# A decoder layer with a product-key expert block: three of four column chunks of v copied into rows, the fourth gathered in place

## The chip, the cores and the metric

The kernel runs on one core of a Trainium2 chip. The metric is the device time in microseconds (us), the median of the runs. The core's engines are TensorE (PE, with its weight loads PEld), VectorE (DVE), ScalarE (ACT), GpSimd (POOL) and SyncE (SP), which issues most of the DMAs; all DMAs run on the same 16 DMA engines.

## The reference, cut to what matters

The layer has 256 tokens of width 2048. A mixer (two kinds of convolution between two projections) and a layer norm give `x1`; then a block of 16384 experts follows, each with a row of `peer_u` and a row of `peer_v` (2048 columns of float32). Each token picks 16 experts in each of 8 heads, 128 in all:

```
q = (x_tok @ w_q).reshape(t, PEER_HEADS, 2, D_HALF)
s = jnp.einsum('thpc,hpnc->thpn', q, sub_keys)
...                                    # top 16 of each half, top 16 of their sums
experts = e1 * N_KEYS + e2
g = jax.nn.softmax(top_s, axis=-1)
act = jax.nn.gelu(jnp.einsum('td,thkd->thk', x_tok, peer_u[experts]))
return jnp.einsum('thk,thkd->td', act * g, peer_v[experts])
```

The result is added to `x1` and normed again.

## The kernel before, in words

**The stream.** All weights pass through TensorE as units of 512 KB (128 partitions x 1024 float32). There are 656 of them in a fixed order: 80 of `w_in` (units 0 to 79), 32 of `w_out`, 32 of `w_q`, 256 of `u` (units 144 to 399, two for each tile of 128 experts) and 256 of `v` (units 400 to 655). SyncE loads them into a ring of four raw slots (`load`, L424 to L428). ScalarE writes a rounded half `w_hi` (L598), a second engine the rest `w_lo = raw - w_hi`: VectorE (L836), or GpSimd (L521) for some units of `w_out` and all from `w_q` to unit 183. Split units have four slots too. TensorE needs both halves: a unit of the stationary kind is 24 matmuls of 256 columns (L1425 to L1427), a unit of `v` 10 of 512 columns (L1592 to L1597). A load waits until the rest of the unit four before it is made (`lo_done`), and `w_hi` waits until TensorE has used that slot (`used`).

**Beside the stream.** In the `w_in` stage VectorE also does the taps of the convolution (L863 to L876), in the `w_out` stage the norms. In the `w_q` stage and the first of `u` it finds the top 16. From tile 20 of `u` on, VectorE builds one-hot tables (L1213 to L1229) from which TensorE makes the gates of 192 tokens, which are multiplied with the activations of all experts.

**The 64 other tokens.** For these the kernel does not multiply with all of `v`. It gathers the picked rows. Two halves of 64 partitions take four heads each, so there are 64 picks (`PICKS`) of 128 rows. This needs three things:
- `act_spill`: the activations of those tokens, written to DRAM during the `u` stage (L723), and gathered one value per partition (`gather_acts`, L556 to L560).
- `v_rows`: `v` in rows, one expert after the other. The `v` that is loaded lies in units: unit `8g + 2j + h` holds column chunk `j` (512 columns of the 2048) of experts `4g + 2h` and `4g + 2h + 1` for each of the 128 first keys, so an expert's row lies in four pieces of 2 KB. SyncE copies it during the earlier stages, DRAM to DRAM, 512 KB a copy in 256 pieces of 2 KB (`copy_unit`, L442 to L446). `copies_by` (L448) spreads the 256 copies evenly over units 12 to 392 of the stream, in the same queue as the loads: after each load `stream` issues the copies that are due.
- The indices: `selections` (L1259 to L1280) computes on VectorE, once, at tile 24 of `u`, the row of `v_rows` and of `act_spill` for each pick.

**The picks.** GpSimd waits for the indices and for all copies, then gathers the row of a pick, 8 KB on each partition, into one of four buffers (`gather_rows`, L546 to L554), and goes on once the pick four before is done. VectorE adds `coef * row` into `picked` (`pick`, L1287 to L1298), 2048 columns at once, at fixed units of the `v` stage (`pick_unit`): 64 picks over units 420 to 622, one each 3.2 units. The act gathers (16 at first, then four for every three picks) stand between the row gathers in the same queue. `picked` is added near the end.

**Extra loads on SyncE's queue.** `x` in its natural layout (2 MB) after unit 15, the output bias (1 MB) after unit 27, the keys (1 MB) after unit 39, the norm weights (2 x 1 MB) after unit 111, and a spilled `x1` (2 MB) and norm weights (2 x 1 MB) in the `v` stage.

Of the kernel before, what the change touches and what calls it, by code (L numbers as in the profile page):

```python
# [5 lines left out]
P = 128  # L6
T = 256
TB = T // P
D = 2048
# [8 lines left out]
N_KEYS = 128  # L18
DCH = 512
NCH = D // DCH  # L20
GROUP = 4
GROUPS = N_KEYS // GROUP
# [11 lines left out]
PICKS = HEADS * TOPK // HALVES  # L34
ROWS = 4
# [25 lines left out]
U_DOWN = U_UP + 2 * N_KEYS  # L61
# [42 lines left out]

V_UNITS = 2 * NCH * GROUPS
COPY0, COPY1 = 12, U_DOWN - 8


def pick_unit(k):
# [18 lines left out]
def build(nc, x_t, x_nat, w_in, w_out, w_q, u_w, v_w, params, sub_keys, b_out, ln1_g, ln1_b, ln2_g, ln2_b, out):  # L130
    f32 = mybir.dt.float32
# [3 lines left out]
    u32 = mybir.dt.uint32  # L135
    ALU = mybir.AluOpType
# [5 lines left out]
    with ctx:  # L142
        def sb(name, shape, dt, where=ctx):
            return where.enter_context(nc.sbuf_tensor(name, shape, dt))
# [114 lines left out]
        rows = [sb(f"rows{i}", [P, D], f32) for i in range(2)] + rows_late  # L259
        stage = sb("stage", [P, STAGE, SPARSE], f32)  # L260
        picked = sb("picked", [P, D], f32)
        sp_sel = sb("sp_sel", [P, 3, PICKS], f32)
        sp_row = sb("sp_row", [P, 3, PICKS], f32)
        sp_idx = sb("sp_idx", [P, 2, PICKS], u32)
        sp_act = sb("sp_act", [P, PICKS], f32)
        sp_coef = sb("sp_coef", [P, PICKS], f32)
        sp_tok = sb("sp_tok", [P, 2], f32)
# [3 lines left out]
        act_dram = nc.dram_tensor("act_spill", [N_KEYS * N_KEYS * SPARSE, 1], f32, kind="Internal").ap()  # L271
        act_tiles = act_dram.rearrange("(c p t) o -> p c (t o)", c=N_KEYS, p=P, t=SPARSE)

        v_rows = nc.dram_tensor("v_rows", [N_KEYS * N_KEYS, D], f32, kind="Internal").ap()
        v_rows_of = v_rows.rearrange("(p g e) (j c) -> p g e j c", p=P, e=2, c=DCH)

        psum = ctx.enter_context(nc.psum_tensor("psum", [P, 8, DCH], f32))
        bank = [psum[:, i, :] for i in range(8)]
# [102 lines left out]
        sp_chain = sem("sp_chain")  # L381
        idx_done = sem("idx_done")
# [4 lines left out]
        rows_in = [sem(f"rows_in{i}") for i in range(ROWS)]  # L387
# [34 lines left out]
        @block.sync  # L422
        def _(sp):
            def load(slot, src, u=None):  # L424

                if u is not None:
                    wait_lo(sp, u - RAW, slot)
                sp.dma_start(raw[:, slot, :], src).then_inc(raw_in[slot], 16)  # L428

            def load_x(c):  # L430
                sp.dma_start(xt_raw[:, 4 * c:4 * c + 4, :], x_t[:, 4 * c:4 * c + 4, :]).then_inc(xt_in[c], 16)

            load(0, w_in[0])
            load_x(0)
            load_x(1)
            load(1, w_in[1])
            load_x(2)
            load_x(3)
            load(2, w_in[2])
            load(3, w_in[3])  # L440

            def copy_unit(n):  # L442

                g, j, h = n // (2 * NCH), n // 2 % NCH, n % 2
                sp.dma_start(v_rows_of[:, 2 * g + h, :, j, :], v_w[n].rearrange("p (e c) -> p e c", c=DCH))\
                    .then_inc(v_copied[n % 2], 16)  # L446

            def copies_by(u):  # L448

                return V_UNITS * min(max(u - COPY0, 0), COPY1 - COPY0) // (COPY1 - COPY0)  # L450

            def stream(src, base, first, end):
                for n in range(first, end):
                    u = base + n
                    load(n % RAW, src[n], u)
                    for m in range(copies_by(u), copies_by(u + 1)):
                        copy_unit(m)


            stream(w_in, 0, RAW, 4 * RAW)  # L460
            sp.dma_start(acc[:, :, :], x_nat.rearrange("(b p) d -> p b d", p=P)).then_inc(xn_in, 16)
            stream(w_in, 0, 4 * RAW, 7 * RAW)
            sp.dma_start(bo[:, :], b_out.to_broadcast([P, D])).then_inc(bo_in, 16)
            stream(w_in, 0, 7 * RAW, 10 * RAW)
            sp.dma_start(keys[:, :], sub_keys).then_inc(keys_in, 16)
            stream(w_in, 0, 10 * RAW, U_OUT)
            stream(w_out, U_OUT, 0, U_Q - U_OUT)

            for dst, src in ((ln_g, ln1_g), (ln_b, ln1_b)):
                sp.dma_start(dst, src.to_broadcast([P, D])).then_inc(ln1_in, 16)  # L470
            stream(w_q, U_Q, 0, 2 * RAW)
            sp.wait_ge(x1_done, TB * NCH)
            sp.dma_start(x1_dram.rearrange("b p d -> p b d"), acc[:, :, :]).then_inc(x1_out, 16)
            stream(w_q, U_Q, 2 * RAW, U_UP - U_Q)
            stream(u_w, U_UP, 0, U_DOWN - U_UP)
            stream(v_w, U_DOWN, 0, 2 * RAW)
            stream(v_w, U_DOWN, 2 * RAW, 16 * RAW)
            sp.wait_ge(x1_out, 16)
            sp.wait_ge(clo_done, 2 * 6)
            sp.dma_start(res[:, :, :], x1_dram.rearrange("b p d -> p b d")).then_inc(res_in, 16)  # L480
            stream(v_w, U_DOWN, 16 * RAW, 24 * RAW)
            sp.wait_ge(clo_done, 2 * 11)
            for dst, src in ((ln2g, ln2_g), (ln2b, ln2_b)):
                sp.dma_start(dst[:, :], src.to_broadcast([P, D])).then_inc(ln2_in, 16)
            stream(v_w, U_DOWN, 24 * RAW, U_LAST - U_DOWN)
            for j in range(NCH):
                for g in range(G_LAST, GROUPS):
                    for h in range(2):
                        u = down_unit(g, j) + h
                        load(u % RAW, v_w[2 * NCH * g + 2 * j + h], u)  # L490
            for n, (b, d) in enumerate(LN2_VECTOR):
                sp.wait_ge(fin, n + 1)
                sp.dma_start(out[b * P:(b + 1) * P, d * DCH:(d + 1) * DCH],
                             res[:, b, d * DCH:(d + 1) * DCH]).then_inc(out_done, 16)
            sp.wait_ge(out_done, 16 * NCH * TB)
# [3 lines left out]
        def _(pool):  # L499
# [46 lines left out]
            def gather_rows(k):  # L546

                if k >= ROWS:
                    pool.wait_ge(picked_done, k - ROWS + 1)
                elif k >= 2:  # L550
                    pool.wait_ge(used, USED0 + U_DOWN)
                nc.gpsimd.indirect_dma_start(  # L552
                    rows[k % ROWS][:, :], None, v_rows,
                    bass.IndirectOffsetOnAxis(sp_idx[:, 1, k:k + 1], 0)).then_inc(rows_in[k % ROWS], 16)  # L554

            def gather_acts(first, end):  # L556
                for k in range(first, end):
# [6 lines left out]
            for done in v_copied:  # L564
                pool.wait_ge(done, 16 * V_UNITS // 2)
            for k in range(2):
                gather_rows(k)
# [257 lines left out]
        def _(dve):  # L825
            tt = nc.vector.tensor_tensor
            ts = nc.vector.tensor_scalar
            stt = nc.vector.scalar_tensor_tensor
# [105 lines left out]
            with dve.Fori(0, CONF_TILES // 2) as i:  # L934
                for b in range(2):
                    u = U_CONF + 8 * i + 4 * (b + 1) + LEAD
# [20 lines left out]
            with dve.Fori(0, SC_TILES // 4) as i:  # L957
                for b in range(4):
                    u = U_SC + 24 * i + 6 * (b + 1) + LEAD
# [146 lines left out]
            for t in range(2 * HEADS):  # L1106
                h, two = t // 2, t % 2
# [51 lines left out]
            for n, (half, b) in enumerate(decodes):  # L1159
                e = eq[n % 2]  # L1160
# [98 lines left out]
            def selections():  # L1259

                n = [0]

                def then(i):
                    n[0] += 1
                    i.then_inc(sp_chain, 1)

                dve.wait_ge(sp_in, 32)
                dve.wait_ge(tok_done, 1)
                dve.wait_ge(fold_made, 3)
                then(ts(sp_tok[:, 1:2], sp_tok[:, 0:1], float(SPARSE), -float(SPARSE), ALU.is_ge, ALU.mult))  # L1270
                then(stt(sp_row[:, 1, :], sp_sel[:, 0, :], float(N_KEYS), sp_sel[:, 1, :], ALU.mult, ALU.add))
                dve.wait_ge(sp_chain, n[0])
                then(tt(sp_tok[:, 0:1], sp_tok[:, 0:1], sp_tok[:, 1:2], ALU.add))
                dve.wait_ge(sp_chain, n[0])
                then(stt(sp_row[:, 0, :], sp_sel[:, 1, :], float(P * SPARSE), sp_tok[:, 0:1].to_broadcast([P, PICKS]),
                         ALU.mult, ALU.add))
                dve.wait_ge(sp_chain, n[0])
                then(stt(sp_row[:, 0, :], sp_sel[:, 0, :], float(SPARSE), sp_row[:, 0, :], ALU.mult, ALU.add))
                dve.wait_ge(sp_chain, n[0])
                nc.vector.tensor_copy(sp_idx[:, :, :], sp_row[:, 0:2, :]).then_inc(idx_done, 1)  # L1280

            def pick_coefs(n):
                sl = slice(PICKS_IN * n, PICKS_IN * (n + 1))
# [3 lines left out]
            def pick(k):  # L1287

                if k % PICKS_IN == 0:
                    pick_coefs(k // PICKS_IN)  # L1290
                dve.wait_ge(coef_done, k // PICKS_IN + 1)
                dve.wait_ge(rows_in[k % ROWS], 16 * (k // ROWS + 1))
                if k == 0:
                    i = ts(picked[:, :], rows[0][:, :], sp_coef[:, 0:1], None, ALU.mult)
                else:
                    dve.wait_ge(picked_done, k)
                    i = stt(picked[:, :], rows[k % ROWS][:, :], sp_coef[:, k:k + 1], picked[:, :], ALU.mult, ALU.add)  # L1297
                i.then_inc(picked_done, 1)  # L1298
# [23 lines left out]
            for c in range((U_ROUTED - LEAD - U_UP) // 2, N_KEYS):  # L1322
                u = U_UP + 2 * c + LEAD
# [29 lines left out]
            for u in range(U_DOWN, U_END):  # L1353
# [11 lines left out]
                j, n = (u - U_LAST) // (2 * LAST), (u - U_LAST) % (2 * LAST)  # L1365
# [341 lines left out]
```

## Time and profile before

| | |
|---|---|
| median of 3 runs | 1885.39 us (1883.87 to 1888.76) |
| profiled execution, its own time | 1880.05 us |
| its span, first to last instruction | 1878.2 us |
| TensorE busy | 1792.3 us, 12082 matmuls |
| VectorE, ScalarE, GpSimd busy | 1366.5, 852.6, 416.8 us |
| moved by DMA | 568.05 MB, mean 302 GB/s |
| HBM read and written | 558.05 MB and 142.61 MB |

The span is about 2 us shorter than the time of its own execution. Busy shares are means over stages with different limits. Matmuls overlap in the record, so TensorE's pace is better read from how many matmuls started in a stretch. "PEclk" is TensorE's granted clock as a part of full speed.

### The profile page before, as it was taken

How to read it: one execution, taken by the hardware profiler on the slowest of the kernel's cores; microseconds unless marked ns; L12 is line 12 of the kernel's file. 1: busy time of each engine (PE TensorE's matmuls, PEld its weight loads, DVE VectorE, ACT ScalarE, POOL GpSimd, SP SyncE). 2: the span in 40 equal slices, each digit the busy share in tenths (PEclk: the TensorE clock that was granted, in tenths of full speed). 3: DMA queues.
4: the chain of work that ended last, by engine and by line, in shares of the span. 5: the costliest groups of instructions: out<-in, count | busy, mean ns of one | idle time of the engine just before them, and what ended most of it. 6: DMA issues, size and time to landing. Idle time of an engine off the chain costs nothing.

```text
span 1878.2 us, 31945 instructions
## 1 busy us (share of the span) xinstructions
PE 1792.3 (95%) x12082; PEld 1632.6 (87%) x12082; DVE 1366.5 (73%) x1891; ACT 852.6 (45%) x1208; POOL 416.8 (22%) x234
## 2 busy tenths in 40 slices
PE   7989899799999999999999999999999899999997
PEld 7989887599999999999999999988777687777775
DVE  7789886569974677777776444457878788878876
ACT  5434335344444444444444444444445444444443
POOL 0000004468894000000000000033444352222101
PEclk9999999999999999999999999999999999999999
DMA  8999898989989999999999999979899999999874
GB/s 274 308 299 290 270 305 260 316 266 292 288 281 303 308 297 292 308 310 299 291 295 298 314 314 311 312 227 332 337 374 357 360 362 350 337 350 348 298 228 135
DMA packets 196386, 568.05 MB, mean 302 GB/s; under 512 B 35344, under 2 KB 35472, under 8 KB 186512
## 3 DMA queue, kind: packets, MB, share of 16 engines
q1 hardware_dynamic: 167072, 494.20, 81.6%
q0 software_dynamic: 11344, 67.67, 9.3%
q10 hardware_dynamic: 17888, 5.26, 1.2%
q8 instruction: 30, 0.49, 0.1%
q14 instruction: 52, 0.43, 0.1%
HBM read 558.05 MB, written 142.61 MB: 373 GB/s over the span
## 4 chain that ended last, share of the span: by engine, by line
PE 40%; DMA 34%; DVE 11%; ACT 6%; issue 6%; POOL 2%; DVEq 0%; POOLq 0%; ACTq 0%; SPq 0%
DMA raw<-in_u_w_dram 16%; DMA raw<-in_v_w_dram 9%; PE psum L1425 8%; PE psum L1426 8%; PE psum L1427 8%; DVE w_lo L836 6%; DMA raw<-in_w_in_dram 6%; ACT w_hi L598 4%; PE psum L1592 3%; PE psum L1593 3%; PE psum L1594 3%; PE psum L1596 3%; PE psum L1597 3%; POOL w_lo L521 2%; DVE picked L1297 2%
## 5 line engine op out<-in xcount | busy, mean ns | idle before, releaser
L598 ACT ACTIVATE w_hi<-raw 128x1024 fp32r<-128x1024 f32 x652 | 691.3, 1061 | 937.5 <-DMA raw<-in_u_w_dram 259.0
L836 DVE TENSOR_TENSOR w_lo<-raw,w_hi 128x1024 fp32r<-128x1024 f32 x568 | 691.0, 1227 | 371.3 <-ACT w_hi L598 361.8
L1425 PE MATMUL psum<-xt_hi,w_hi 128*128 128x256 f32 x2944 | 834.3, 283 | 35.6 <-DVE w_lo L836 15.1
L1426 PE MATMUL psum<-xt_lo,w_hi 128*128 128x256 f32 x2944 | 826.9, 281 | 0.0
L1427 PE MATMUL psum<-xt_hi,w_lo 128*128 128x256 f32 x2944 | 826.3, 281 | 0.0
L1425 PEld LDWEIGHTS psum<-xt_hi,w_hi 128*128 128x128 f32 x2944 | 558.4, 190 | 42.2 <-issue 17.6
L1426 PEld LDWEIGHTS psum<-xt_lo,w_hi 128*128 128x128 f32 x2944 | 558.5, 190 | 0.0
L1427 PEld LDWEIGHTS psum<-xt_hi,w_lo 128*128 128x128 f32 x2944 | 558.2, 190 | 0.0
L552 POOL DMA_INDIRECT rows<-v_rows,sp_idx x64 | 106.8, 1668 | 922.2 <-DMA v_rows<-in_v_w_dram 615.6
L521 POOL TENSOR_TENSOR w_lo<-raw,w_hi 128x1024 fp32r<-128x1024 f32 x82 | 210.8, 2583 | 86.4 <-ACT w_hi L598 85.8
L1592 PE MATMUL psum<-w_hi,c_hi 128*128 128x512 f32 x504 | 203.5, 404 | 20.6 <-DVE w_lo L836 17.9
L1593 PE MATMUL psum<-w_lo,c_hi 128*128 128x512 f32 x504 | 200.6, 398 | 0.0
L1594 PE MATMUL psum<-w_hi,c_lo 128*128 128x512 f32 x504 | 200.3, 397 | 0.0
L1597 PE MATMUL psum<-w_lo,c_both 128*128 128x512 f32 x504 | 200.1, 397 | 0.0
L1596 PE MATMUL psum<-w_hi,c_both 128*128 128x512 f32 x504 | 200.0, 397 | 0.0
L1297 DVE SCALAR_TENSOR_TENSOR picked<-rows,sp_coef,picked 128x2048 f32<-128x2048 f32 x63 | 147.9, 2348 | 0.1
L1592 PEld LDWEIGHTS psum<-w_hi,c_hi 128*128 128x128 f32 x504 | 95.4, 189 | 53.5 <-DVE w_lo L836 27.7
L1594 PEld LDWEIGHTS psum<-w_hi,c_lo 128*128 128x128 f32 x504 | 95.5, 189 | 23.2
L1596 PEld LDWEIGHTS psum<-w_hi,c_both 128*128 128x128 f32 x504 | 95.4, 189 | 23.3 <-DVE w_lo L836 0.2
L1597 PEld LDWEIGHTS psum<-w_lo,c_both 128*128 128x128 f32 x504 | 95.1, 189 | 23.0
L1593 PEld LDWEIGHTS psum<-w_lo,c_hi 128*128 128x128 f32 x504 | 95.6, 190 | 21.8
L875 DVE SCALAR_TENSOR_TENSOR cacc<-apad,prm,cacc x232 | 101.2, 479 | 0.0
(182 smaller groups left out, 1148.6 us busy)
## 6 DMA issues: line engine op xcount, KB each, us to landing
v_rows<-in_v_w_dram SPq DMA_DIRECT2D x256, 512.0 KB, 9.4
raw<-in_u_w_dram SPq DMA_DIRECT2D x256, 512.0 KB
raw<-in_v_w_dram SPq DMA_DIRECT2D x256, 512.0 KB
raw<-in_w_in_dram SPq DMA_DIRECT2D x80, 512.0 KB
raw<-in_w_out_dram SPq DMA_DIRECT2D x32, 512.0 KB
raw<-in_w_q_dram SPq DMA_DIRECT2D x32, 512.0 KB
act_spill<-stage ACTq DMA_DIRECT2D x32, 128.0 KB, 10.1
xt_raw<-in_x_t_dram SPq DMA_DIRECT2D x4, 512.0 KB, 8.0
```

Of the source, the lines that this page charges most:

```text
L521: nc.gpsimd.tensor_tensor(w_lo[s][:, :], raw[:, s, :], w_hi[s][:, :].bitcast(f32), ALU.subtract).then_inc(lo_done[s], SPLIT)
L598: nc.scalar.activation(parts_of(slot_u)[0][:, :], raw[:, slot_u % RAW, :], ACT.Copy).then_inc(hi_done, 1)
L836: tt(lo_w[:, :], raw[:, slot_u % RAW, :], hi_w[:, :].bitcast(f32), ALU.subtract).then_inc(lo_done[slot_u % SPLIT], SPLIT)
L1297: i = stt(picked[:, :], rows[k % ROWS][:, :], sp_coef[:, k:k + 1], picked[:, :], ALU.mult, ALU.add)
L1425: mm(dst, hi_w[:, sl], xt_hi[:, kk, :], start=st, stop=False)
L1426: mm(dst, hi_w[:, sl], xt_lo[:, kk, :], start=False, stop=False)
L1427: i = mm(dst, lo_w[:, sl], xt_hi[:, kk, :], start=False, stop=en)
L1592: mm(v_bank(j, 0), hi_c[:, n, :], w1, start=st, stop=False)
L1593: mm(v_bank(j, 0), hi_c[:, n, :], w2, start=False, stop=False)
L1594: i = mm(v_bank(j, 0), lo_c[:, n, :], w1, start=False, stop=en)
L1596: mm(v_bank(j, 1), both_c[:, n, :], w1, start=st, stop=False)
L1597: i = mm(v_bank(j, 1), both_c[:, n, :], w2, start=False, stop=en)
```

## The change

Chunk 3 of `v` is no longer copied. `v_rows` holds 1536 columns (6 KB) per expert instead of 2048, and 192 copies instead of 256 are spread over units 24 to 392 instead of 12 to 392. Each pick is gathered by two indirect DMAs on GpSimd: 6 KB per partition out of `v_rows`, and 2 KB per partition out of the units of `v` themselves (`v_ends`, the units seen as rows of 512 columns). `selections` computes a third index for it, `(8g + 6 + h) * 256 + 2 * e1 + e` with `e2 = 4g + 2h + e`, by bit masks. Both gathers of a pick count on one semaphore, so VectorE waits for 32 instead of 16.

```diff
-V_UNITS = 2 * NCH * GROUPS
-COPY0, COPY1 = 12, U_DOWN - 8
+JOINED = NCH - 1
+V_UNITS = 2 * JOINED * GROUPS
+COPY0, COPY1 = 24, U_DOWN - 8
...
-        v_rows = nc.dram_tensor("v_rows", [N_KEYS * N_KEYS, D], f32, kind="Internal").ap()
+        v_rows = nc.dram_tensor("v_rows", [N_KEYS * N_KEYS, JOINED * DCH], f32, kind="Internal").ap()
         v_rows_of = v_rows.rearrange("(p g e) (j c) -> p g e j c", p=P, e=2, c=DCH)
+        v_ends = v_w.rearrange("u p (e c) -> (u p e) c", c=DCH)
...
-                g, j, h = n // (2 * NCH), n // 2 % NCH, n % 2
-                sp.dma_start(v_rows_of[:, 2 * g + h, :, j, :], v_w[n].rearrange("p (e c) -> p e c", c=DCH))\
+                g, j, h = n // (2 * JOINED), n // 2 % JOINED, n % 2
+                sp.dma_start(v_rows_of[:, 2 * g + h, :, j, :],
+                             v_w[2 * NCH * g + 2 * j + h].rearrange("p (e c) -> p e c", c=DCH))\
                     .then_inc(v_copied[n % 2], 16)
...
                 nc.gpsimd.indirect_dma_start(
-                    rows[k % ROWS][:, :], None, v_rows,
+                    rows[k % ROWS][:, 0:JOINED * DCH], None, v_rows,
                     bass.IndirectOffsetOnAxis(sp_idx[:, 1, k:k + 1], 0)).then_inc(rows_in[k % ROWS], 16)
+                nc.gpsimd.indirect_dma_start(
+                    rows[k % ROWS][:, JOINED * DCH:D], None, v_ends,
+                    bass.IndirectOffsetOnAxis(sp_idx[:, 2, k:k + 1], 0)).then_inc(rows_in[k % ROWS], 16)
...
+                then(nc.vector.tensor_copy(sp_u[:, 0, :], sp_sel[:, 1, :]))
...
+                then(nc.vector.tensor_single_scalar(sp_u[:, 1, :], sp_u[:, 0, :], 1, ALU.bitwise_and))
+                then(nc.vector.tensor_single_scalar(sp_u[:, 2, :], sp_u[:, 0, :], 2, ALU.bitwise_and))
...
+                then(nc.vector.tensor_single_scalar(sp_u[:, 0, :], sp_u[:, 0, :], N_KEYS - GROUP, ALU.bitwise_and))
+                dve.wait_ge(sp_chain, n[0])
+                then(nc.vector.tensor_copy(sp_f[:, :, :], sp_u[:, :, :]))
+                dve.wait_ge(sp_chain, n[0])
+
+                then(stt(sp_row[:, 2, :], sp_f[:, 0, :], float(2 * NCH * 2 * P // GROUP), sp_f[:, 1, :],
+                         ALU.mult, ALU.add))
...
+                then(stt(sp_row[:, 2, :], sp_f[:, 2, :], float(P), sp_row[:, 2, :], ALU.mult, ALU.add))
...
+                then(stt(sp_row[:, 2, :], sp_sel[:, 0, :], 2.0, sp_row[:, 2, :], ALU.mult, ALU.add))
+                dve.wait_ge(sp_chain, n[0])
+                then(nc.vector.tensor_scalar_add(sp_row[:, 2, :], sp_row[:, 2, :], float(2 * JOINED * 2 * P)))
+                dve.wait_ge(sp_chain, n[0])
+                nc.vector.tensor_copy(sp_idx[:, :, :], sp_row[:, 0:3, :]).then_inc(idx_done, 1)
...
-                dve.wait_ge(rows_in[k % ROWS], 16 * (k // ROWS + 1))
+                dve.wait_ge(rows_in[k % ROWS], 32 * (k // ROWS + 1))
```

## Rows read from the trace of the kernel before

**Rows 1.** The page, part 1: busy us, share of the span, instructions.

```profile
PE 1792.3 (95%) x12082; PEld 1632.6 (87%) x12082; DVE 1366.5 (73%) x1891; ACT 852.6 (45%) x1208; POOL 416.8 (22%) x234
```

**Rows 2.** Windows: stretch, length, busy us of each engine (instructions), PEclk, DMA share, GB/s.

```profile
700.00:1000.00 300.00, 299.96 (x2574) 297.10 (x2573) 217.09 (x287) 143.77 (x289) 0.00 (x0) 1.00 0.99 301
1000.00:1200.00 200.00, 199.04 (x1695) 198.01 (x1695) 98.61 (x112) 84.34 (x140) 0.00 (x0) 1.00 1.01 305
1300.00:1800.00 500.00, 480.21 (x2016) 379.28 (x2014) 401.75 (x320) 235.45 (x256) 158.39 (x104) 0.99 0.92 344
```

**Rows 3.** Windows of 40 us, engines in the order PE, PEld, DVE, ACT, POOL.

```profile
40.00:80.00 40.00, 38.10 (x309) 37.54 (x308) 32.20 (x59) 17.36 (x18) 0.00 (x0) 0.96 0.99 298
80.00:120.00 40.00, 37.07 (x310) 36.27 (x309) 32.71 (x58) 17.15 (x18) 0.00 (x0) 1.00 1.01 315
120.00:160.00 40.00, 36.24 (x288) 35.28 (x287) 34.74 (x56) 14.00 (x17) 0.00 (x0) 0.96 0.98 291
...
200.00:240.00 40.00, 34.19 (x265) 33.58 (x264) 32.36 (x61) 15.03 (x17) 0.00 (x0) 0.91 0.86 273
...
600.00:640.00 40.00, 39.10 (x337) 38.65 (x336) 27.20 (x42) 19.06 (x37) 0.00 (x0) 1.00 0.99 311
640.00:680.00 40.00, 37.99 (x310) 37.23 (x309) 26.07 (x38) 18.48 (x38) 0.00 (x0) 0.96 0.98 297
```

**Rows 4.** Chain of waits, 84 to 142 us: start, us, what.

```profile
105.04 10.10 DMA raw<-in_w_in_dram
...
119.13 1.15 DVE w_lo L836
120.30 10.31 DMA raw<-in_w_in_dram
```

**Rows 5.** Windows: one slice of the down stage.

```profile
1530.00:1560.00 30.00, 30.00 (x130) 24.17 (x129) 24.37 (x21) 14.21 (x16) 13.58 (x11) 1.00 0.99 382
```

**Rows 6.** DMA issues: count, KB of each, median us from issue to landing.

```profile
v_rows<-in_v_w_dram SPq DMA_DIRECT2D x256, 512.0 KB, 9.4
...
acc<-in_x_nat_dram SPq DMA_DIRECT2D x1, 2048.0 KB, 11.0
```

**Rows 7.** Timeline of VectorE near 205 us: start, us, line, [idle before <-releaser].

```profile
205.32 1.23 DVE L836 TENSOR_TENSOR w_lo<-raw,w_hi 128x1024 fp32r<-128x1024 f32 x1 [0.84 <-ACT w_hi L598]
212.48 0.48 DVE L966 SCALAR_TENSOR_TENSOR scpad<-psum,prm,hval 128x256 f32<-128x256 f32 x1 [5.94 <-issue]
```

**Rows 8.** Waits, 340 to 358 us, then 1190 to 1210: us, times, longest.

```profile
PE psum L1469 <- POOL w_lo L521: 2.7, 2, 1.7
...
PE psum L1425 <- ACT psum L714: 2.5, 1, 2.5
```

**Rows 9.** Timelines of ScalarE and TensorE near 652 us.

```profile
650.97 1.06 ACT L598 ACTIVATE w_hi<-raw 128x1024 fp32r<-128x1024 f32 x1 [3.68 <-DMA raw<-in_u_w_dram]
...
654.74 1.83 PE L1559 MATMUL psum<-oh2g,oh 128*128 128x256 f16 x8 [2.01 <-DVE oh2g L1229]
```

**Rows 10.** Groups (busy us, mean ns, idle before, releaser); last, one line's starts.

```profile
L552 POOL DMA_INDIRECT rows<-v_rows,sp_idx x64 | 106.8, 1668 | 922.2 <-DMA v_rows<-in_v_w_dram 615.6 <-DVE picked L1297 291.1 <-DVE picked L1294 13.6
L558 POOL DMA_INDIRECT sp_act<-act_spill,sp_idx x64 | 81.6, 1275 | 56.2 <-DMA act_spill<-stage 30.1 <-issue 26.2
L1297 DVE SCALAR_TENSOR_TENSOR picked<-rows,sp_coef,picked 128x2048 f32<-128x2048 f32 x63 | 147.9, 2348 | 0.1
...
L1297 DVE SCALAR_TENSOR_TENSOR picked<-rows,sp_coef,picked x63: 2336/2346/2398, 1289.7 to 1782.2; 128x2048 f32<-128x2048 f32 x63
```

**Rows 11.** The page, part 3: queue, packets, MB, share of 16 engines.

```profile
q1 hardware_dynamic: 167072, 494.20, 81.6%
q0 software_dynamic: 11344, 67.67, 9.3%
```

**Rows 12.** One index operation: ns min/median/max, first and last start.

```profile
L1278 DVE SCALAR_TENSOR_TENSOR sp_row<-sp_sel,sp_row x1: 224/224/224, 628.3 to 628.3; 128x64 f32<-128x64 f32 x1
```

**Rows 13.** Timeline of GpSimd: the eighth act gather, [idle before <-releaser].

```profile
1251.93 1.32 POOL L558 DMA_INDIRECT sp_act<-act_spill,sp_idx  x1 [3.35 <-issue]
```

More of the change, by code:

```diff
@@ L263, in build @@
         sp_row = sb("sp_row", [P, 3, PICKS], f32)
-        sp_idx = sb("sp_idx", [P, 2, PICKS], u32)
+        sp_u = sb("sp_u", [P, 3, PICKS], u32)
+        sp_f = sb("sp_f", [P, 3, PICKS], f32)
+        sp_idx = sb("sp_idx", [P, 3, PICKS], u32)
         sp_act = sb("sp_act", [P, PICKS], f32)
@@ L1277, in selections @@
                 dve.wait_ge(sp_chain, n[0])
+                then(stt(sp_row[:, 2, :], sp_f[:, 2, :], float(P), sp_row[:, 2, :], ALU.mult, ALU.add))
                 then(stt(sp_row[:, 0, :], sp_sel[:, 0, :], float(SPARSE), sp_row[:, 0, :], ALU.mult, ALU.add))
                 dve.wait_ge(sp_chain, n[0])
-                nc.vector.tensor_copy(sp_idx[:, :, :], sp_row[:, 0:2, :]).then_inc(idx_done, 1)
+                then(stt(sp_row[:, 2, :], sp_sel[:, 0, :], 2.0, sp_row[:, 2, :], ALU.mult, ALU.add))
[3 more added lines that the diff above has]
+                nc.vector.tensor_copy(sp_idx[:, :, :], sp_row[:, 0:3, :]).then_inc(idx_done, 1)
             def pick_coefs(n):
```

## The prediction

> **What bounds the kernel now.** I read the engine table first. TensorE is busy 95% of the span, so it sets the end, and a change that does not touch its work can win only the time that it stands waiting or runs slow [rows 1]. That share flatters it, because matmuls overlap in the record, so the next view is the number of matmuls per stretch. From 700 to 1000 us, 2574 matmuls started in 300 us, one per 116.6 ns, with the DMA engines at a share of 0.99 [rows 2]. This is the full pace for a 256-column matmul: TensorE has no idle time there although the DMA engines are full. The same view in 40 us slices shows where it falls short of the 343 matmuls that fit at that pace: 309, 310 and 288 from 40 to 160 us, 265 from 200 to 240, 337 and 310 from 600 to 680 [rows 3]. From 1000 to 1200 us it is 1695 of 1716 [rows 2].
>
> The chain of waits says what is late. In the early stretch it is a ring: a load takes 10.10 us from 105.04 on, ScalarE splits the unit, VectorE does taps and then its own half of the split (1.15 us at 119.13), that frees the raw slot, and the next load starts at 120.30 and takes 10.31 us [rows 4]. The ring has four slots, so it feeds a unit each (120.30 - 105.04) / 4 = 3.8 us here, and TensorE wants one each 24 x 0.1166 = 2.8 us. Two thirds of a turn are the load. The loads are slow because the copies stand in the same queue. All 256 copies are 512 KB each, so as many bytes as 256 loads, spread over 380 units (0.67 per unit).
>
> In the down stage there are no copies. 2016 matmuls of 512 columns started from 1300 to 1800 us, and at the 130 per 30 us of the best slice 2167 would fit: 151 x 0.2308 = 34.8 us are lost there, at a DMA share of 0.92 [rows 2, 5].
>
> **Copies: 192 for 256, from unit 24 on.** Per unit this is 192/368 = 0.52 for 0.67. Bytes per unit with its load fall from 1.67 to 1.52 times 512 KB, 9%. With the share at 0.99 and TensorE at full pace before, I expect about 0.9 and loads that arrive ahead, so that up to three split units lie ready and cover a late load. The stretches, one by one:
> - 40 to 160 us: 34 + 33 + 55 = 122 matmuls, 14.2 us [rows 3]. By unit 48 (about 140 us) the copies issued are 24 x 0.52 = 12.5 instead of 36 x 0.67 = 24.3. The 12 that are gone are 6.2 MB, at 298 GB/s some 21 us of the DMA engines. What they were in conflict with are the one-off loads of x (2 MB) [rows 6], the bias and the keys (1 MB each), 4.2 MB or 14 us. So the cause is more than covered. I take 9 us and keep 0 and 14.2: VectorE is over 80% busy here and some gaps are its own.
> - 200 to 240 us: 78 matmuls, 9.1 us, with a low clock in part (0.91). VectorE issued nothing for 5.94 us before its first operation of the next loop [rows 7], released by nothing that the profile shows. The copies did not cause that, but TensorE felt it whole because no split unit was in store. With loads ahead it may be hidden; I take 3, ends 0 and 9.1.
> - 340 to 358 us: TensorE waits 2.7 us for splits of w_out whose loads were late [rows 8]. I take 1.
> - 600 to 680 us: 6 + 33 matmuls, 4.5 us. At 650.97 a split starts after 3.68 us of waiting for a load, the one-hot behind it on VectorE is late, and TensorE waits 2.01 us for it at 654.74 [rows 9]. 1000 to 1200 us: 21 matmuls, 2.4 us. Near 1204 a late load holds back the GELU behind it on ScalarE and TensorE waits 2.5 us [rows 8]. Together 9.4, I take 6.
> - Startup, the layer norms, the stretch where GpSimd splits (500 to 600 us) and the 300 us at full pace: nothing.
> Sum 9 + 3 + 1 + 6 = 19 us of at most 14.2 + 9.1 + 2.7 + 9.4 = 35.4.
>
> **The second gather per pick.** 64 more indirect DMAs, each 128 pieces of 2 KB, while the first shrinks to 6 KB: the same bytes.
> - On GpSimd: 64 x (1.67 + 0.30) = 126 us. One pick then costs 2 x 1.97 + 4/3 x (1.28 + 0.30) = 6.0 us of GpSimd [rows 10], while picks come every 492.5 / 62 = 7.9 us [rows 10]. Queued behind each gather are the next act gathers, and VectorE waits for both. GpSimd waited 291 us for picks before, which hides all 126; gathers run three picks (24 us) ahead and VectorE stood idle 0.1 us before all picks together. Cost 0 while this cover holds, otherwise the slow rival below.
> - On the DMA engines: the bytes do not change, the pieces do. Queue 0 (the gathers) took 9.3% x 16 x 1878.2 = 2795 us for 67.67 MB in 11344 packets, queue 1 took 24522 us for 494.20 MB in 167072 [rows 11]. If the whole difference per MB is a cost per packet, it is 49 ns; 64 x (128 + 16) = 9216 further packets are then 450 us, 28 us of all 16 engines, and the share in the down stage would rise from 0.92 to 0.98. The slice at 0.99 ran at full pace [rows 5]. The other end is below nothing: smaller pieces let load packets in between, and at most the 34.8 us lost there could come back. I take a cost of 2 us, near that slice's 0, and keep +28 and -34.8.
>
> The Trainium skill bears on both points, and nothing above or below rests on it. "DMA: Bandwidth & Descriptors", section Specifications, gives 512 B as the smallest transfer at line rate, so 2 KB pieces would cost nothing more and the sum would be 19 instead of 17 us; by the fit of rows 11 taken whole it would be a loss of 9 instead. Its section on the anatomy of one DMA speaks against the change: each software DMA carries a fixed 2.0 us besides its bytes. If that stood on VectorE's path it would be 128 us, so slower by some 110; no run here shows it, and the row with 0.1 us of idle time before the picks says that it is hidden.
>
> **VectorE's indices.** Nine further operations of the kind that took 0.22 us (64 columns) [rows 12], about 2 us once, near 628 us. VectorE waits for ScalarE there; I take 0, ends 0 and 2. The SP queue gets 64 fewer issues; its issue was never what a load waited for.
>
> **Sum.** The profiled execution took 1880.05 us (span 1878.2 and 1.85 around it). 1880.05 - 19 + 2 = 1863. It lay 5.3 us below the median of the three runs, 1885.39, so the forecast on that scale is 1868.4.
>
> **Rivals.**
> - *The copies cost nothing where it counts* (0.22). For it: the 300 us at full pace with the DMA engines full; the 5.94 us with no releaser and the norms are not theirs. Only a few early gaps close, 3 us: 1882. Against: in the early stretch the chain is made of loads of ten us.
> - *All of it comes back* (0.10). Three units in store cover the VectorE stall too, and low-clock stretches that follow idle time vanish with it: 1885.4 - 35.4 = 1850.
> - *Slower: the GpSimd queue falls behind* (0.10). After seven act gathers in a row GpSimd stood 3.35 us with no releaser before the next [rows 13], as if only so many DMAs may be outstanding. With 3.33 per pick instead of 2.33 this is 3.35 x 3.33 / 7 = 1.6 us, and 7.6 of 7.9 us are used. Row gathers drain slower than four-byte ones; if the stall is twice as long a pick costs 9.2 us. It decides from 7.9 us on. Price: 1.3 us for the 36 picks that carry act gathers, 47, less the lead of 24, gives 23 us on VectorE and so on TensorE: 1885.4 - 19 + 23 = 1889. The packets at 49 ns and no cover would end near there too.
> - That the copies don't get fewer cannot be; the counts are in the code.
>
> **Chances.** Forecast 0.58 (its own range 1860 to 1878), rivals 0.22, 0.10, 0.10. About 0.3%, 5.7 us, can be told from no change here: faster is 0.58 + 0.10 = 0.68, same 0.22, slower 0.10. The range reaches to the all-back case and the slow one, 1852 to 1889.
>
> **What the new profile would show.** DMA share from 700 to 1000 us near 0.9 with TensorE still at 2574 matmuls; 40 to 160 us above 980 matmuls instead of 907; landings of the copies below the 9.4 us median [rows 6]; 1300 to 1800 us at 2000 or more matmuls; GpSimd busy about 107 us longer; VectorE still hardly idle before picks. It would be wrong if the early slices stay at their counts with faster loads (then VectorE bounds them), or if the down stage loses more than 50 matmuls.

## The result and the profile after

Median 1836.02 us after (4 runs, 1829.45 to 1839.67), 1885.52 us before (4 runs, 1883.87 to 1888.76): ratio 0.9732, 95% interval 0.9701 to 0.9762. The profiled execution took 1829.45 us, its span 1827.6. The forecast was 1868.4 with a range from 1852 to 1889: right in sign, but it had 17 us of gain for 49.5 measured, too small by a factor of almost three, and the time lies below the range. One execution of the kernel before, of 4504 us, fell in a slower state of the chip and is left out of all ratios below.

The page of the changed kernel, parts 1, 3 and 4 [rows 1, 11]:

```profile
PE 1773.9 (97%) x12082; PEld 1623.4 (89%) x12082; DVE 1365.2 (75%) x1900; ACT 853.1 (47%) x1208; POOL 504.1 (28%) x298
...
q1 hardware_dynamic: 149664, 460.64, 72.3%
q0 software_dynamic: 16464, 67.68, 9.8%
...
PE 76%; DMA 9%; DVE 7%; issue 4%; ACT 2%; POOL 1%; DVEq 0%; POOLq 0%; SPq 0%; ACTq 0%
```

The last line is the chain that ended last. The kernel before had on the same line:

```profile
PE 40%; DMA 34%; DVE 11%; ACT 6%; issue 6%; POOL 2%; DVEq 0%; POOLq 0%; ACTq 0%; SPq 0%
```

A third of the old chain was the landing of loads; now three quarters of the chain are TensorE itself. The same windows as before [rows 2, 3]:

```profile
40.00:80.00 40.00, 40.00 (x342) 40.00 (x341) 36.94 (x69) 19.99 (x22) 0.00 (x0) 1.00 0.74 264
80.00:120.00 40.00, 40.00 (x342) 40.00 (x341) 37.88 (x62) 18.78 (x21) 0.00 (x0) 1.00 0.90 329
120.00:160.00 40.00, 40.00 (x342) 40.00 (x342) 39.10 (x73) 17.20 (x20) 0.00 (x0) 1.00 0.86 299
...
700.00:1000.00 300.00, 300.00 (x2575) 297.46 (x2575) 214.86 (x278) 143.37 (x282) 0.00 (x0) 1.00 0.82 276
1000.00:1200.00 200.00, 200.00 (x1658) 197.31 (x1657) 99.72 (x111) 89.30 (x144) 12.33 (x11) 1.00 0.83 279
1300.00:1800.00 500.00, 481.62 (x2023) 381.85 (x2022) 397.81 (x323) 236.95 (x256) 207.28 (x142) 0.99 0.90 332
```

(1000 to 1200 us now holds the first units of `v`, whose matmuls are twice as wide.) The early slices stand at the full 342 matmuls. At TensorE's full pace the DMA share (the mean busy share of the 16 DMA engines) is 0.82; it was 0.99, and I had expected about 0.9. The landing of a copy, the time from its issue to its end, fell from 9.4 us [rows 6] to 5.2:

```profile
v_rows<-in_v_w_dram SPq DMA_DIRECT2D x192, 512.0 KB, 5.2
```

Where the 50.6 us of span came from, by the first and last starts of TensorE's lines in both traces:

| point of the program | before | after | won since the last point |
|---|---|---|---|
| first matmul of `w_out` | 260.1 | 237.5 | 22.6 |
| first transpose of `x1` | 361.5 | 332.0 | 6.9 |
| first scores | 387.9 | 354.1 | 4.3 |
| first gate batch | 598.4 | 562.1 | 2.5 |
| last gate batch | 1012.2 | 970.5 | 5.4 |
| last matmul of `u` | 1233.1 | 1185.9 | 5.5 |
| last matmul of `v` | 1867.3 | 1816.7 | 3.4 |

### The profile page after: what moved, and what is told of

It reads as the page before. It is cut to its first block, busy times and chain, and to the rows that moved or that the text cites. A ratio compares the mean times of both kernels' runs of the same rounds, so it can differ in the third digit from the quotient of the medians.

```text
span 1827.6 us, 31954 instructions
## 1 busy us (share of the span) xinstructions
PE 1773.9 (97%) x12082; PEld 1623.4 (89%) x12082; DVE 1365.2 (75%) x1900; ACT 853.1 (47%) x1208; POOL 504.1 (28%) x298
## 3 DMA queue, kind: packets, MB, share of 16 engines
q0 software_dynamic: 16464, 67.68, 9.8%
## 4 chain that ended last, share of the span: by engine, by line
PE 76%; DMA 9%; DVE 7%; issue 4%; ACT 2%; POOL 1%; DVEq 0%; POOLq 0%; SPq 0%; ACTq 0%
PE psum L1449 19%; PE psum L1450 18%; PE psum L1451 18%; DMA raw<-in_v_w_dram 8%; PE psum L1616 3%; PE psum L1618 3%; PE psum L1617 3%; DVE w_lo L845 3%; PE psum L1620 3%; PE psum L1621 3%; ACT w_hi L607 1%; PE psum L1583 1%; DVE picked L1321 1%; PE psum L1493 1%; PE psum L1495 1%
## 5 line engine op out<-in xcount | busy, mean ns | idle before, releaser
L558 POOL DMA_INDIRECT rows<-v_rows,sp_idx x64 | 109.0, 1703 | 789.2 <-DMA v_rows<-in_v_w_dram 598.9
L567 POOL DMA_INDIRECT sp_act<-act_spill,sp_idx x64 | 85.7, 1340 | 67.6 <-issue 36.3
```

## The experiments

Ratios are against the kernel before on the same chip. There its medians were 1880 to 1886 us and its single executions 1868 to 1893, so kernels of different rows are compared by their ratios, and a few us between two medians tell nothing. Shares and landings are from one trace each. "Share" and GB/s are the DMA engines' from 700 to 1000 us, "landing" is the copies' median.

| kernel | median us | ratio, 95% interval | share, GB/s | landing us |
|---|---|---|---|---|
| before | 1885.52 | | 0.99, 301 | 9.4 |
| after | 1836.02 | 0.9732 (0.9701 to 0.9762) | 0.82, 276 | 5.2 |
| e1, all 256 copies, two gathers | 1834.44 | 0.9722 (0.9675 to 0.9769) | 0.88, 304 | 5.8 |
| e2, 192 copies from unit 12 | 1837.26 | 0.9738 (0.9692 to 0.9784) | 0.82, 274 | 5.3 |
| e3, before, copies from unit 24 | 1903.95 | 1.0110 (1.0074 to 1.0147) | 0.99, 295 | 10.4 |
| e4, 192 copies, one gather | 1835.66 | 0.9732 (0.9684 to 0.9780) | 0.83, 277 | 5.3 |
| e8, as e4, pieces 1 MB apart | 1839.80 | 0.9799 (0.9759 to 0.9839) | 0.88, 277 | 6.2 |
| e9, before, 1 MB + 8 KB apart | 1836.69 | 0.9772 (0.9726 to 0.9818) | 0.89, 304 | 5.7 |
| e10, before, 8 KB apart | 1832.46 | 0.9759 (0.9712 to 0.9805) | 0.90, 305 | 5.8 |
| e5, no copies, one gather | 1831.84 | 0.9756 (0.9721 to 0.9790) | 0.57, 184 | |
| e7, 128 copies, three gathers | 1850.58 | 0.9870 (0.9825 to 0.9915) | 0.75, 245 | 5.2 |
| e13, e10 with 320 copies | 1840.23 | 0.9755 (0.9726 to 0.9785) | 0.96, 330 | 6.5 |
| e11, after, extras cut up | 1826.68 | 0.9718 (0.9688 to 0.9748) | 0.82, 276 | 5.3 |
| e12, e10, extras cut up | 1833.08 | 0.9761 (0.9729 to 0.9794) | 0.90, 303 | 5.9 |

**e1: undo the smaller number.**

```diff
-V_UNITS = 2 * JOINED * GROUPS
-COPY0, COPY1 = 24, U_DOWN - 8
+V_UNITS = 2 * NCH * GROUPS
+COPY0, COPY1 = 12, U_DOWN - 8
...
+                sp.dma_start(v_rows_of[:, 2 * g + h, :, j, :] if j < JOINED else v_last_of[:, 2 * g + h],
```

> The changed kernel with all 256 copies back, from unit 12 on; the fourth chunk is copied into a tensor of its own that nothing reads, and is still gathered in place. Theory (fewer copies are the whole gain: with 0.67 copies per unit the ring of loads is late, with 0.52 it runs ahead): the time goes back to 1885, within 1875 to 1895, and the DMA share from 700 to 1000 us back to 0.99. Rival (the narrower rows and the gather in place give it): stays at 1836 to 1850.

Measured: 1834 us, all of the gain with all 256 copies. My theory, that fewer copies are the whole gain, fell here. (A fourth of the copies goes out in 128 pieces of 4 KB, 256 KB apart, instead of 256 pieces of 2 KB, so this run alone did not prove the rival. These copies landed after 5.6 us, the others after 5.8.)

**e2 and e3: the start.** The one line `COPY0, COPY1 = 24, U_DOWN - 8` to 12 in the changed kernel, and the reverse in the kernel before.

> The changed kernel with its 192 copies spread from unit 12 instead of 24. Theory (number per unit decides, 0.505 is no more than 0.52): 1836 to 1842. Rival (the late start of the copies gives the first 11 us, those of units 0 to 32): 1847 or more.

> The kernel before with its 256 copies spread from unit 24 instead of 12, 0.70 per unit instead of 0.67. Theory (number per unit decides): 1878 to 1890, what is gained up to unit 24 is given back later. Rival (late start): 1865 to 1875.

Measured: 1837 and 1904 us. e2 came out as expected. e3 missed both ranges: in the old layout the late start costs 1.1%. Its first `w_out` matmul starts 8.2 us earlier than before (251.9 for 260.1) and its last of `u` 19.9 later (1253.0 for 1233.1). With 0.70 copies per unit for 0.67 the DMA engines no longer keep up with TensorE:

```profile
700.00:1000.00 300.00, 289.81 (x2460) 285.67 (x2460) 208.53 (x276) 137.60 (x277) 0.00 (x0) 0.99 0.99 295
```

Here, at the same share of 0.99, TensorE starts 2460 matmuls for 2574 [rows 2]. In that stretch the kernel before had stood on the very edge.

**e4: take the second gather away.**

```diff
-                    rows[k % ROWS][:, :], None, v_rows,
+                    rows[k % ROWS][:, :], None, v_flat,
```

on the kernel before with 192 copies from unit 24 and rows of 6 KB; `v_flat` is the units of `v` seen as rows of 8 KB. The rows it picks are not the experts' rows: e4, e8 and e5 leave that part of the computation out.

> The kernel before with 192 copies from unit 24 and rows of 6 KB, but one gather of 8 KB per pick, out of the units of v as they lie in memory; the rows picked are not the experts' rows, so that part of the computation is left out. Against the changed kernel this takes away only the second gather and the 6 KB + 2 KB pieces. Theory (the second gather is hidden): 1832 to 1840, as the changed kernel. Rival (its packets or GpSimd's time cost part of the gain): 1815 to 1828. Rival (smaller pieces help the loads of the down stage): 1842 to 1850.

Measured: 1836 us, so the second gather and its smaller pieces cost nothing that can be told.

**e8, e9, e10: where the pieces are written.** A copy writes 256 pieces, those of neighbouring first keys 128 rows apart: 1 MB with rows of 8 KB, 768 KB with rows of 6 KB. That was the other thing the diff changed. e8 is e4 with rows of 8 KB. e9 and e10 leave 256 copies and one gather and change only the place. (e9 also fills the padding once with two more copies, and its index counts 129 rows per first key.)

```diff
# e9
-        v_rows = nc.dram_tensor("v_rows", [N_KEYS * N_KEYS, D], f32, kind="Internal").ap()
+        v_rows = nc.dram_tensor("v_rows", [N_KEYS * (N_KEYS + 1), D], f32, kind="Internal").ap()
...
# e10
-        v_rows_of = v_rows.rearrange("(p g e) (j c) -> p g e j c", p=P, e=2, c=DCH)
+        v_rows_of = v_rows.rearrange("(g e p) (j c) -> p g e j c", p=P, e=2, c=DCH)
...
-                then(stt(sp_row[:, 1, :], sp_sel[:, 0, :], float(N_KEYS), sp_sel[:, 1, :], ALU.mult, ALU.add))
+                then(stt(sp_row[:, 1, :], sp_sel[:, 1, :], float(N_KEYS), sp_sel[:, 0, :], ALU.mult, ALU.add))
```

> The kernel with 192 copies and one gather of 8 KB out of v's units (its rows are not the experts' rows, so that part of the computation is left out), but the rows that are written are 8 KB again, so the pieces for neighbouring first keys lie 1 MB apart as before and not 768 KB. Theory 1 (fewer copies are enough by themselves): 1832 to 1848. Theory 2 (only the place where the pieces are written matters): 1870 or more.

> The kernel before with one row of 8 KB of padding after the 128 rows of each first key, the padding filled once by two more copies of 512 KB: all 256 copies, one gather, pieces of neighbouring first keys 1 MB + 8 KB apart instead of 1 MB. Theory 2 (a distance of exactly 1 MB between the 128 pieces of a copy makes copies and loads slow): 1832 to 1842 and a landing of the copies near 6 us instead of 9.4. Theory 1 alone (only the number of copies counts), or that the 8 KB rows as such are at fault: 1878 to 1890.

> The kernel before with v_rows ordered by the second key first, so that the rows of neighbouring first keys lie side by side: all 256 copies, one gather, no padding, pieces 8 KB apart and each copy within 2 MB. Theory 2 (the 1 MB distance): 1832 to 1842. If any large power of two as distance is bad, 8 KB too: 1860 or more. Theory 1 alone: 1878 to 1890.

Measured: 1840, 1837 and 1832 us, each within the range of the theory that it was to test. Either is enough alone for all or nearly all of the gain: 192 copies at 1 MB, or 256 copies at another distance. (The ratio of e8, 0.9799, is 0.7% above the changed kernel's; its four executions run from 1832 to 1845 us, and whether fewer copies at 1 MB give a little less isn't settled.) The windows of e8, then e9, show what each is worth to the DMA engines at the same pace of TensorE:

```profile
700.00:1000.00 300.00, 300.00 (x2575) 297.46 (x2575) 214.79 (x278) 143.47 (x282) 0.00 (x0) 1.00 0.88 277
```

```profile
700.00:1000.00 300.00, 300.00 (x2575) 297.46 (x2575) 214.75 (x279) 143.37 (x282) 0.00 (x0) 1.00 0.89 304
```

At 276 or 277 GB/s the share is 0.88 with 1 MB and 0.82 without: 0.06 for the distance. At 301 to 305 GB/s it is 0.99 and 0.89 or 0.90. And 256 for 192 copies is 0.07 or 0.08 at the good distances (0.82 to 0.89 or 0.90), 0.11 at 1 MB (0.88 to 0.99).

**e5: no copies at all.** `V_UNITS = 0`, gather from `v_flat`.

> The kernel before without any copy, one gather of 8 KB per pick out of v's units (its rows are not the experts' rows, so that part of the computation is left out). It bounds what less DMA traffic before the v stage can bring. Theory (with the loads ahead TensorE is the limit, nothing is left to win): 1822 to 1834, within 10 us of the changed kernel. Rival (each copy taken away brings more): 1800 to 1815.

Measured: 1832 us. From a share of 0.90 down nothing that can be told is left to win: e5 is level with e9 and e10 on the same chip (ratios 0.9756 for 0.9772 and 0.9759).

**e13: fill the DMA engines in the good layout.**

```diff
                         copy_unit(m)
+                        if m // 2 % NCH == 0:
+                            copy_again(m)
```

> The kernel before with v_rows ordered by the second key first (pieces 8 KB apart, 1832 us with a DMA share of 0.90 at full pace) and 64 more copies of 512 KB: the copies of chunk 0 are made a second time, into a tensor that nothing reads, right after the first. 320 copies, 0.84 per unit. Theory (what costs is that the DMA engines are full at TensorE's full pace, however they come to be full): the share from 700 to 1000 us is 0.96 or more and the time rises to 1845 to 1890. Rival (the 1 MB distance hurts the loads in a way of its own, and load on the DMA engines as such does not): 1832 to 1840, with the same early stretches as the kernel ordered by the second key.

Measured: 1840 us, 5 us below the range of the theory and at the upper end of the rival's. The share is what the theory asked for:

```profile
700.00:1000.00 300.00, 300.00 (x2576) 297.46 (x2574) 216.67 (x281) 143.15 (x285) 0.00 (x0) 1.00 0.96 330
```

Neither is shown by it. The early stretches are slower than in e10, against the rival: the first `w_out` matmul comes at 242.1 us (235.3 in e10) and the last of `u` at 1194.8 (1185.1; 1183 to 1191 in all other kernels with a share of 0.90 or less). But over the whole the ratio, 0.9755, is that of e10, 0.9759: the `v` stage of this trace was 7 us shorter (629.6 for 636.2). So a share of 0.96 cost at most some us. Whether the engines being full is the whole cost of the old layout, or the 1 MB distance delays loads besides, stays open. More bytes than before are carried (330 for 301 GB/s) at a time 2.4% shorter: bytes alone did not fill the old queue.

**e7: one chunk further.** `JOINED = NCH - 2` and a third gather per pick.

> The change carried one chunk further: two chunks copied (128 copies), two gathered in place, so three gathers per pick on GpSimd. A pick then costs GpSimd 3 x (1.70 + 0.30) + 4/3 x (1.34 + 0.30) = 8.2 us while picks come every 7.9. Theory (only what exceeds the interval counts, 0.3 us for 36 picks, and the lead of 24 us covers it; the copies bring nothing more): 1832 to 1842. Rival from the prediction (a stall after every seven DMAs, 3.7 x 4.33 / 7 = 2.3 us more per pick, 10.5 in all): 36 x 2.6 less 24 is 70 us, 1895 or more, with VectorE idle before its picks.

Measured: 1851 us, 1.4% slower than the changed kernel by the two ratios, between both expectations. The groups of the picks on VectorE and of its second gather on GpSimd:

```profile
L1326 DVE SCALAR_TENSOR_TENSOR picked<-rows,sp_coef,picked 128x2048 f32<-128x2048 f32 x63 | 148.2, 2353 | 33.8 <-issue 17.0 <-DMA rows<-in_v_w_dram,sp_idx 16.5 <-DVE sp_coef L1314 0.2
...
L561 POOL DMA_INDIRECT rows<-in_v_w_dram,sp_idx x64 | 85.7, 1340 | 59.6 <-issue 59.6
```

VectorE now stands idle 33.8 us before its picks, 16.5 of them put down to the landing of rows and 17.0 to nothing that the profile shows. GpSimd stands 59.6 us before this gather with no releaser, 40 more than 64 times the 0.30 us that lie between two gathers. The `v` stage takes 647.2 us for 630.8. The slow rival of the prediction came true one gather later than I placed it; what GpSimd stands for, no run shows.

**e11 and e12: a try at a faster version.** In the changed kernel TensorE starts 793 matmuls from 1300 to 1500 us, behind the one-off loads of 2 MB:

```profile
1300.00:1500.00 200.00, 190.60 (x793) 152.29 (x792) 155.12 (x124) 91.69 (x99) 117.41 (x82) 0.97 0.94 356
```

Both kernels cut these into 16 DMAs of 256 KB with four stream loads after each:

```diff
-            sp.dma_start(res[:, :, :], x1_dram.rearrange("b p d -> p b d")).then_inc(res_in, 16)
-            stream(v_w, U_DOWN, 16 * RAW, 24 * RAW)
+            for n in range(8):
+                b, sl = n // NCH, slice(n % NCH * DCH, (n % NCH + 1) * DCH)
+                sp.dma_start(res[:, b, sl], x1_dram[b, :, sl]).then_inc(res_in, 16)
+                stream(v_w, U_DOWN, (16 + n) * RAW, (17 + n) * RAW)
```

> The changed kernel with the one-off loads of the down stage cut up: the 2 MB of spilled x1 as 8 DMAs of 256 KB and the 2 MB of norm weights as 8, each followed by four loads of the stream. In the changed kernel's trace TensorE loses 14.9 us from 1300 to 1350 and 1400 to 1450 us, behind a load that took 12.7 us just after the 2 MB. Theory (a burst in the queue of a stage with a DMA share of 0.9 is what starves the ring): 1820 to 1829. Rival (the bytes are the same and the stage is at its limit anyway): 1832 to 1840.

> The kernel before with v_rows ordered by the second key first (256 copies, one gather) and the one-off loads cut up in the same way. Theory: 1820 to 1829, the same as the changed kernel with the loads cut up. If the separate gather of 2 KB helps the down stage, it is slower than that by 3 us or more.

Measured: 1827 and 1833 us. Locally it works, here the same 200 us in e11:

```profile
1300.00:1500.00 200.00, 191.94 (x811) 150.81 (x810) 161.26 (x128) 93.49 (x101) 114.84 (x84) 1.00 0.97 363
```

18 matmuls more are 4 us, and the granted clock there is 1.00 for 0.97. Over the whole, 0.9718 against 0.9732 and 0.9761 against 0.9759 lie within each other's intervals: e11 has the lowest median of all, but that it beats the changed kernel isn't shown. e12 missed its range, and by the rule that I had set for it (3 us or more slower than e11) the second gather would help the `v` stage. The traces do not bear that out (628.1 us for it in e11, 630.2 in e12), nor does e4, so it stays open.

## Why the prediction was wrong

**The wait and the path were right:** loads that land late feed a ring of four slots too slowly, and TensorE, the bound, loses time only where no split unit is in store. The chain (DMA 34% to 9%) and the plateau fit it: all but one of the kernels with a share of 0.90 or less take 1827 to 1840 us, and the exception, e7, loses its time at the gathers. What relieves the loads was right only in part: I had the number of the copies and not their distance.

**The step that failed is the term for the copies, 19 us of at most 35.4.** By the table above it measured 47.2 us up to the last matmul of `u`. It was mis-sized in two ways, and a part of both is the clock.
- *I cut what I had found.* Of the `w_in` stage I took 9 + 3 of 23.3 us, for fear that VectorE bounds it; it gave 22.6. In the new trace VectorE is busy 39.10 of 40 us from 120 to 160 us with TensorE at its full 342. Busy is not late. The idle time of VectorE between two loops, of which I wrote that the copies did not cause it, fell from 5.94 us [rows 7] to 2.86. It is 5.68 us in e3, the other kernel at a share of 0.99, between 2.7 and 4.7 in all with fewer copies or another distance, and 2.43 in e5 without copies. So half of it or more went with the DMA traffic; what the engine does in it, no run shows. What is left is covered by units in store:

```profile
189.59 0.48 DVE L975 SCALAR_TENSOR_TENSOR scpad<-psum,prm,hval 128x256 f32<-128x256 f32 x1 [2.86 <-issue]
```

- *I left out what I took for fixed.* `w_out` and the first norm gave 11.2 us for the 1 that I took (at most 2.7), the stretch up to the first gate batch 2.5 for 0. The norm hung on a load too. The chain of the kernel before, and then its VectorE:

```profile
354.38 12.61 DMA raw<-in_w_q_dram
367.02 1.06 ACT w_hi L598
...
368.20 0.16 DVE L912 RECIPROCAL rstd<-rstd 128x1 f32<-128x1 f32 x1 [3.67 <-ACT rstd L675]
```

  On ScalarE the small step of the norm (L675, at 367.98) stood behind a split that waited for its load of 12.61 us. In the changed kernel the same step of VectorE has no wait before it, and TensorE's idle time before the transposes of `x1` fell from 14.5 to 7.7 us. The late part of `u` gave 10.9 us for 6 (at most 9.4).
- *The clock.* The granted clock over the span rose from 0.987 to 0.993. With levels of 2.4 and 1.2 GHz that is 49 us at the lower level before and 26 after, at half the pace some 11 us of the gain (an estimate from these two figures). It is no further amount but lies inside the stretches above. My counts held the part within my windows, not the one where TensorE stands idle around the norm, which in part remains (before, then after):

```profile
360.00:400.00 40.00, 29.39 (x217) 27.78 (x216) 22.43 (x68) 15.10 (x23) 22.16 (x10) 0.87 0.84 267
```

```profile
320.00:360.00 40.00, 32.71 (x208) 29.22 (x207) 25.04 (x57) 15.93 (x23) 19.93 (x9) 0.91 0.77 286
```

The "all of it comes back" rival (0.10) was the nearest, and even it stopped at 35.4, because it added up only the windows that I had picked. I had not counted the matmul starts of the other stretches against their full pace.

**What I overlooked in the diff.** The rows narrowed from 8 to 6 KB, which moved the pieces of a copy from 1 MB to 768 KB apart. Another distance alone gives a gain of the same size (e1, e9, e10). My share of about 0.9 was right for the number of copies: e8, with 192 of them at 1 MB, shows 0.88; the distance made it 0.82. That does not explain the missed gain, though: e8 gives nearly all of it too. The Trainium skill, "DMA: Bandwidth & Descriptors", section "Latency and other measured facts", says that copies whose partitions lie a large power of two apart run slower (its figures are for 512 KiB and from 2 MiB on, with pieces of 16 KiB), and that a few KiB of padding restore them. By that rule the traces agree: 8 KB of padding after each megabyte took the share from 0.99 at 301 GB/s to 0.89 at 304. That a distance of 8 KB, a power of two as well, is harmless (0.90 at 305) is measured here. What in the memory causes it, no run shows.

**The second gather: right.** GpSimd's gathers cost 109.0 + 81.5 us for 106.8 [rows 10], so 84 more for my 107 to 126; VectorE stood idle 0.1 us before its picks, and e4 is equal to the changed kernel. I took 2 us on the DMA engines; queue 0 went from 9.3% [rows 11] to 9.8% of a shorter span, 2866 for 2795 us, so about 71 us more (the shares are rounded to 0.1%, 29 us) and not the 450 of the upper bound; it counts 5120 packets more (16464 for 11344) and not the 9216 that I had worked out, some 14 ns each for my 49 at most. The `v` stage took 630.8 us for 634.2 (last matmul less last of `u`), and 633 to 641 in e1, e2, e4, e8, e9 and e10, so the difference is scatter.

**The index work: right.** Nine operations more (1900 for 1891), no effect seen.

**The slow rival** priced stops that are real but expected them to bind one gather too early: at two gathers GpSimd still waited 176.7 us for picks, at three 50.5.

What stays open is how the gain of this change divides between fewer copies and their place. Both suffice alone, so it has no single answer; on the DMA share they are worth 0.07 to 0.11 and 0.06 to 0.10.

## What to carry to other kernels

Where a shared queue is full at the bound engine's full pace, look for the losses in every late start that hangs on it, also those behind small steps of an engine that works in order; count the bound engine's starts over the whole trace against its full pace, take that as the upper end of the gain, and argue about what will not come back. Here, once the queue had a tenth to spare, taking more from it brought nothing. And when a diff changes the shape of a tensor in memory, work out the distance between the pieces of one DMA before and after: an exact megabyte cost 0.06 to 0.10 of the DMA share here, and one row of padding (e9) or another order of the rows, two lines changed (e10), removed it.

## What the runs showed of the hardware that I had not expected

- DRAM to DRAM copies in 2 KB pieces 1 MB apart, beside a stream of loads: share 0.99 for 301 GB/s; 1 MB + 8 KB or 8 KB apart: 0.89 and 0.90 for 304 and 305 GB/s.
- Between a share of 0.57 and 0.90 the time hardly moved (1827 to 1840 us, e7 aside); at 0.96 it was 1840 with the same ratio, at 0.99 it was 1886, and 1904 when 3% more copies per unit were asked for.
- VectorE's idle time at the change from one loop to the next, with no releaser in the profile, was longest where the DMA engines were full: 5.94 and 5.68 us at a share of 0.99, 2.7 to 4.7 at 0.75 to 0.96 (in no strict order), 2.43 at 0.57.
- In the first sixteen act gathers GpSimd stood still after the seventh and the fourteenth: 3.35 and 4.25 us before, 3.67 and 4.44 us after, with no releaser that the profile shows. With three row gathers per pick stops without a releaser reached 5.5 us, and the whole became 1.4% slower.
- A gather of 128 pieces of 2 KB beside one of 6 KB cost the DMA engines 2866 us of engine time for 2795 with one gather of 8 KB, over 64 picks.
